# Expert gates scattered into a DRAM table by accumulating DMAs, and the up tiles' weights split on ScalarE and VectorE

## The reference, cut to what matters

```python
s1 = einsum('nhd,hkd->nhk', q[..., :half], k1)      # 128 row keys
s2 = einsum('nhd,hkd->nhk', q[..., half:], k2)      # 128 column keys
v1, i1 = top_k(s1, 16);  v2, i2 = top_k(s2, 16)
cand = v1[..., :, None] + v2[..., None, :]          # 256 candidates of a head
cidx = i1[..., :, None] * 128 + i2[..., None, :]
sv, pos = top_k(cand, 16)
idx = take_along_axis(cidx, pos)                    # 16 experts of a head
gate = softmax(sv)
act = gelu(einsum('nd,nhkd->nhk', h, u[idx]))
y = einsum('nhk,nhkd->nd', gate * act, v[idx])
```

## Time and profile before

| | |
|---|---|
| median of 3 runs | 2392.8 us (2392.65 to 2400.04) |
| profiled execution | 2399.22 us |
| its span, first to last instruction | 2397.4 us |
| mean granted clock of PE | 0.975 |
| busy: PE, PEld, DVE, ACT, POOL | 2316.3, 2238.5, 1566.4, 796.7, 1176.5 us |
| first up matmul, first down matmul, last down matmul | 860.6, 1764.3, 2380.2 us |

### The profile page before, as it was taken

How to read it: one execution, slowest core, us unless ns; L and a number is a source line. 1 busy time by engine, 2 the same in 40 slices (tenths; PEclk the granted TensorE clock), 3 DMA queues, 4 the chain that set the end, 5 groups by cost and what they waited for, 6 DMA issues and landing times.

```text
span 2397.4 us, 42364 instructions
## 1 busy us (share of the span) xinstructions
PE 2316.3 (97%) x15368; PEld 2238.5 (93%) x15368; DVE 1566.4 (65%) x2881; ACT 796.7 (33%) x1433; POOL 1176.5 (49%) x710
## 2 busy tenths in 40 slices
PE   7999999999999999999998999999999999999997
PEld 7899989898999999999998999999999999999996
DVE  6423723697765489999302777777657777787777
ACT  3212320564110011111112666666633332333332
POOL 4444341254554446666654444444454555565642
PEclk9999996899999999999998999999999999999998
DMA  6345345356554446663333444444489999999973
GB/s 199 117 143 156 117 134 184 109 162 216 181 187 145 140 148 206 210 193 127 129 128 135 151 178 179 179 179 179 179 301 308 312 331 306 339 309 332 316 253 129
DMA packets 318702, 475.27 MB, mean 198 GB/s; under 512 B 18448, under 2 KB 229008, under 8 KB 314784
## 3 DMA queue, kind: packets, MB, share of 16 engines
q1 hardware_dynamic: 185536, 256.47, 33.2%
q10 hardware_dynamic: 110560, 150.56, 18.6%
q0 software_dynamic: 22528, 67.19, 8.0%
HBM read 392.75 MB, written 148.52 MB: 226 GB/s over the span
## 4 chain that ended last, share of the span: by engine, by line
PE 83%; DVE 10%; issue 2%; ACT 2%; DMA 1%; ACTq 1%; POOL 0%; DVEq 0%; SPq 0%; POOLq 0%
PE ps L469 50%; PE ps L743 25%; PE ps L716 2%; PE ps L626 1%; PE ps L571 1%; PE ps L618 1%; DMA sr<-sig_scratch 1%; PE ps L675 1%; DVE xpad L1365 1%; ACT oh L1047 0%; DVE rstd L1449 0%; DVE rstd L1427 0%; PE ps L596 0%; DVE rr L1415 0%; PE ps L508 0%
## 5 line engine op out<-in xcount | busy, mean ns | idle before, releaser
L416 POOL TENSOR_SCALAR w_hi<-w_raw 128x1024 fp32r<-128x1024 f32 x225 | 261.9, 1164 | 901.3 <-issue 669.3
L419 POOL TENSOR_TENSOR w_lo<-w_raw,w_hi 128x1024 fp32r<-128x1024 f32 x225 | 579.6, 2576 | 18.8
L469 PE MATMUL ps<-n_hi,w_hi 128*128 128x288 f32 x2048 | 439.2, 296 | 7.7 <-DVE n_lo L1186 3.7
L469 PE MATMUL ps<-n_lo,w_hi 128*128 128x288 f32 x2048 | 439.4, 296 | 0.0
L469 PE MATMUL ps<-n_hi,w_lo 128*128 128x288 f32 x2048 | 439.0, 295 | 0.0
L743 PE MATMUL ps<-c_hi,w_lo 128*128 128x448 f32 x1024 | 371.7, 363 | 0.0
L743 PE MATMUL ps<-c_lo,w_hi 128*128 128x448 f32 x1024 | 371.1, 362 | 0.0
L743 PE MATMUL ps<-c_hi,w_hi 128*128 128x448 f32 x1024 | 368.9, 360 | 1.2 <-issue 0.8
L469 PEld LDWEIGHTS ps<-n_hi,w_hi 128*128 128x128 f32 x2048 | 327.0, 189 | 9.3 <-issue 4.8
L469 PEld LDWEIGHTS ps<-n_hi,w_lo 128*128 128x128 f32 x2048 | 330.7, 189 | 0.0
L469 PEld LDWEIGHTS ps<-n_lo,w_hi 128*128 128x128 f32 x2048 | 329.8, 189 | 0.0
(11 more groups left out here) (276 smaller groups left out, 3748.5 us busy)
## 6 DMA issues: line engine op xcount, KB each, us to landing
value_rows<-in_down SPq DMA_DIRECT2D x128, 512.0 KB, 5.3
w_raw<-in_up SPq DMA_DIRECT2D x128, 512.0 KB, 3.4
w_raw<-in_down SPq DMA_DIRECT2D x128, 512.0 KB, 6.6
w_raw<-in_trunk SPq DMA_DIRECT2D x96, 512.0 KB, 3.4
act_scratch<-ast ACTq DMA_DIRECT2D x128, 288.0 KB, 2.1
c_act<-act_scratch ACTq DMA_DIRECT2D x16, 1792.0 KB, 18.3
gate_scratch<-gst ACTq DMA_DIRECT2D x28, 1024.0 KB, 4.3
c_gate<-gate_scratch ACTq DMA_DIRECT2D x15, 1792.0 KB, 25.8
```

What stands on the lines that cost most here:

```text
L416: nc.gpsimd.tensor_scalar(w_hi[j % 2][:, :, :], w_raw[j][:, :, :], 1.0, 1.0, ALU.mult, ALU.mult).then_inc(w_hi_done, 1)
L419: nc.gpsimd.tensor_tensor(w_lo[j % 2][:, :, :], w_raw[j][:, :, :], f(w_hi[j % 2][:, :, :]), ALU.subtract).then_inc(w_split, 1)
L469: last = nc.tensor.matmul(ps[:, 2 * p + a, 0:w], wt[:, k, :], act[:, k, t0 + a * w:t0 + (a + 1) * w], start=k == 0 and part == 0, stop=k = ...
```

## The change

- **A cleared table.** POOL sets a tile of zeros once, and SP clears the table of gates (448 tokens x 16,384 experts, float32, 29.4 MB; now one row of 448 tokens for each expert) with 32 DMAs behind the loads and copies of trunk tiles 64 to 95.
- **Scatter.** The numbers of the cells are worked out by DVE (`cells`), and POOL adds each gate into the table by an indirect DMA with accumulation: one DMA for a chunk of tokens and one pick, 4 chunks x 128 picks = 512 DMAs (the fourth chunk has 64 tokens). Between the heads of a chunk POOL waits for the earlier head's DMAs to land; the chunks are staggered by three heads.
- **No expansion.** Transposes, one-hots, `gate_pair`, `gated`, `low_parts`, the 28 stores and the direct fill of `c_gate` go.
- **Splitting.** POOL splits tiles up to 105 (N_B = 106) alone. From tile 106 on ACT makes the high part and DVE the low part, as was done for the down tiles.
- **Top-k.** Chunk 0 runs as before; each of chunks 1 to 4 is interleaved with the low parts of 16 up tiles, and softmax and cells of the chunk before it are made inside. ACT makes the exponential chunk by chunk, behind the Gelu of up tiles 11, 27, 43, 59 and 75.
- **Loads.** ACT waits for all scatters behind up tile 119, and then loads the gates of the first two groups. A group's gates are now read as 8 rows of 448 numbers in one piece for each partition.

```diff
-            with pool.Fori(1, N_D // 4) as i:
+            with pool.Fori(1, N_CLEAR // 4 - 1) as i:
                 for j in range(4):
                     split(j, i * 4 + j)
+            pool.wait_ge(sig_stored, 16 * 3 * KT)
+            nc.gpsimd.memset(zeros[:, :], 0.0).then_inc(zeroed, 1)
...
+            def clear(k):
+                sp.dma_start(g_rows[:, ds(k * 4, 4), :], zeros[:, :].unsqueeze(1).to_broadcast([P, 4, TD])
+                             ).then_inc(cleared, 16)
+            def load_up(j, n):
+                sp.wait_ge(d_lo_done, n - (N_B + 3))
+                sp.dma_start(w_raw[j][:, :, :], up[ds(n - N_U, 1), :, :]...).then_inc(raw_in[j], 16)
...
+            def scatter_gates(c, h):
+                w = P if c < CD - 1 else DLAST
+                if h:
+                    pool.wait_ge(scattered[c], 16 * TOPK * h)
+                else:
+                    pool.wait_ge(cells_ready, c + 1)
+                for m in range(h * TOPK, (h + 1) * TOPK):
+                    nc.gpsimd.indirect_dma_start(
+                        g_cells, bass.IndirectOffsetOnAxis(ap=g_idx[0:w, c, m:m + 1], axis=0),
+                        chosen[0:w, c, 2, m:m + 1], None, compute_op=ALU.add).then_inc(scattered[c], 16)
...
+            pool.wait_ge(cleared, 16 * (NK // 4))
+            for step in range(PH + 3 * (CD - 1)):
+                for c in range(CD):
+                    if 0 <= step - 3 * c < PH:
+                        scatter_gates(c, step - 3 * c)
...
+            def split_high(j, n):
+                act.wait_ge(raw_in[j], (n - j) * 4 + 16)
+                act.wait_ge(tile_done, n - 1)
+                A(w_hi[j % 2][:, :, :], w_raw[j][:, :, :], ACT.Copy).then_inc(d_hi_done, 1)
...
+            begin = (N_B - 2 - N_U) // 4
+            up_tiles(0, begin, split=False)
+            for c in range(CT):
+                up_tiles(begin if c == 0 else 4 * c - 1, 4 * c + 3)
+                act.wait_ge(picked, c + 1)
+                A(chosen[:, c, 2, :], chosen[:, c, 2, :], ACT.Exp).then_inc(gate_exp, 1)
+            up_tiles(4 * CT - 1, NK // 4 - 2)
...
             act_load(0, 0)
+            for c in range(CD):
+                act.wait_ge(scattered[c], 16 * PICKS)
+            gate_load(0, 0)
+            gate_load(1, 1)
+            up_tiles(NK // 4 - 2, NK // 4 - 1)
...
+            def split_low(j, n):
+                dve.wait_ge(d_hi_done, n - (N_B - 1))
+                V.tensor_tensor(w_lo[j % 2][:, :, :], w_raw[j][:, :, :], f(w_hi[j % 2][:, :, :]), ALU.subtract
+                                ).then_inc(d_lo_done, 1)
+            def cells(i, then):
+                row = lambda side: chosen[:, ds(i, 1), side, :].rearrange("p o j -> p (o j)")
+                then(V.scalar_tensor_tensor(cell_f[:, :], row(1), float(NK), row(0), ALU.mult, ALU.add))
+                then(V.scalar_tensor_tensor(cell_f[:, :], cell_f[:, :], float(TD),
+                                            token[:, ds(i, 1)].to_broadcast([P, PICKS]), ALU.mult, ALU.add))
+                then(V.tensor_copy(g_idx[:, ds(i, 1), :].rearrange("p o j -> p (o j)"), cell_f[:, :]))
...
+            choose(0, 0, lambda: None)
+            with dve.Fori(1, CT) as i:
+                choose(i, i * STEPS + (FIRST_STEPS - STEPS), next_low, i - 1)
```

More of the change, by code:

```diff
@@ L55 @@
 NGB = TD // GB
[L56 to L59, removed]
 E1G = 8
@@ L386, in _ @@
                     copy_rows(i * 4 + (j - 4))
-            with sp.Fori(0, (NGRP * KT - N_U) // 4 + 1) as i:
+            sp.wait_ge(zeroed, 1)
+            with sp.Fori(N_CLEAR // 4, N_U // 4) as i:
+                for j in range(4):
+                    load(trunk, i, 0, j)
+                    copy_rows(i * 4 + (j - 4))
+                    clear(i * 4 + (j - N_CLEAR))
+            first_up = (N_B + 3 - N_U) // 4
+            with sp.Fori(0, first_up) as i:
                 for j in range(4):
@@ L698, in _ @@
             hn2 = lambda j: (n_hi, n_lo)
[L700 to L723, removed]
-                for j in range(4):
[L725 to L733, removed]
+            split_at = (N_B - N_U) // 4
+            stage(N_U, split_at * 4, hn2)
+            for j in range(4):
+                n = N_U + split_at * 4 + j
+                pe.wait_ge(pair_free[j % 2], n // 2 + 1)
+                product(j, n, n_hi, n_lo, j % 2, by_pool=n < N_B)
+            with pe.Fori(split_at + 1, NK // 4) as i:
+                for j in range(4):
+                    pe.wait_ge(pair_free[j % 2], i * 2 + (N_U // 2 + j // 2 + 1))
+                    product(j, i * 4 + (N_U + j), n_hi, n_lo, j % 2, by_pool=False)
             def down_tile(d, n, gg, ready=None, begin=False, end=False):
-                pe.wait_ge(d_lo_done, n - (N_D - 1))
+                pe.wait_ge(d_lo_done, n - (N_B - 1))
                 s = d % 2
@@ L1013, in _, with up_tile @@
             act.wait_ge(sc_copied, 3 * PH + 1)
-            def up_tiles(i0, i1, before=None, after=None):
+            def split_high(j, n):
+                act.wait_ge(raw_in[j], (n - j) * 4 + 16)
+                act.wait_ge(tile_done, n - 1)
+                A(w_hi[j % 2][:, :, :], w_raw[j][:, :, :], ACT.Copy).then_inc(d_hi_done, 1)
+            def up_tile(j, u):
+                act.wait_ge(tile_done, u + (N_U + 1))
+                act.wait_ge(a_stored[j], (u - j) * 4 + 16)
+                A(halves(ast[j][:, :]), opair(j % 2), ACT.Gelu).then_inc(pair_free[j % 2], 1)
@@ L1022, in up_tiles @@
[L1022 to L1056, removed]
-                        gated(q % RING, i * 2 * BQ + q)
@@ L1529, in _, with softmax, choose @@
             LOWEST = -3.4028235e38
-            STEPS = 21
-            with dve.Fori(0, CT) as i:
+            FIRST_STEPS, STEPS = 21, 27
+            def split_low(j, n):
+                dve.wait_ge(d_hi_done, n - (N_B - 1))
+                V.tensor_tensor(w_lo[j % 2][:, :, :], w_raw[j][:, :, :], f(w_hi[j % 2][:, :, :]), ALU.subtract
+                                ).then_inc(d_lo_done, 1)
+            V.tensor_tensor(cell_f[:, :], idt[:, :], iot[:, :], ALU.mult).then_inc(cell_step, 1)
+            dve.wait_ge(cell_step, 1)
+            V.tensor_reduce(token[:, 0:1], cell_f[:, :], AX, ALU.add).then_inc(cell_step, 1)
+            dve.wait_ge(cell_step, 2)
+            for c in range(1, CD):
+                V.tensor_scalar(token[:, c:c + 1], token[:, 0:1], float(c * P), None, ALU.add).then_inc(cell_step, 1)
+            dve.wait_ge(cell_step, CD + 1)
+            def softmax(i, then):
+                parts = chosen[:, ds(i, 1), 2, :].rearrange("p o (h k) -> p (o h) k", h=PH)
+                then(V.tensor_reduce(sm[:, 0, :], parts, AX, ALU.add))
+                then(V.reciprocal(sm[:, 0, :], sm[:, 0, :]))
+                then(V.tensor_tensor(parts, parts, sm[:, 0, :].unsqueeze(2).to_broadcast([P, PH, TOPK]), ALU.mult))
+            def cells(i, then):
[4 more added lines that the diff above has]
+                then(V.tensor_copy(g_idx[:, ds(i, 1), :].rearrange("p o j -> p (o j)"), cell_f[:, :]))
+            def choose(i, done, low, earlier=None):
                 n_top = [0]
@@ L1545, in best @@
                     then(last)
+                    low()
                     for q in range(n):
@@ L1557, in best @@
                     then(last)
+                    low()
                 then(V.tensor_copy(work[:, :, :], scores[:, ds(i, 1), :, :].rearrange("p o q k -> p (o q) k")))
                 best(2 * PH, lambda q: work[:, q, :], lambda q, s: tv[:, q, s:s + 8], lambda q, s: ti[:, q, s:s + 8])
+                if earlier is not None:
+                    dve.wait_ge(gate_exp, earlier + 1)
+                    softmax(earlier, then)
+                    cells(earlier, then)
+                    dve.sem_inc(cells_ready, 1)
+                    low()
                 V.tensor_copy(tif[:, :, :], ti[:, :, :])
```

241 lines of the change are left out of this document (105 added, 136 removed).

## The result

The changed kernel took 2650.97 us (median of 4 runs, 2648.28 to 2653.4) beside 2394.84 for the kernel before (4 runs, 2392.65 to 2400.04): ratio 1.107, 95% interval 1.104 to 1.109. It is slower by a tenth; the forecast was 2329 us, and its range ended at 2474.

The account below looks back on a forecast made before the run. PE, busy 97% of the span, was taken as the bound. From 2399.2 us profiled, 80 off PE and 16 added for standstill and lower clock gave 2335, or 2329 for the median; forecast 2313 to 2353, upward range to 2474.

Parts of the forecast that it names:

- the price of an accumulating DMA: POOL's scatter: each accumulating DMA costs a gather's 0.94 us undisturbed, 1.24 us rhythm, 1.37 us mean, ending at 1674 us.
- stretching: POOL's scatter: DMAs starting inside DVE operations with two SBUF inputs wait for them, 1.47 us a DMA during the top-k.
- The rival that came true: POOL's scatter: accumulating DMAs cost more than gathers, so it ends late and eats the gain; up to 2474 us, chance 0.25.
- Its bound: Upper price for POOL's scatter DMAs: the down stage's mean, 1.61 us each, PE standing 153 us, 2474 us total.
- Landings in series: POOL's scatter: each DMA waits for the one before to land, 3.9 us each; above 3600 us, chance 0.03.
- The 64-row DMAs: Fourth chunk's 128 scatter DMAs: save 60 us if the price goes by rows, nothing if it is fixed.
- What leaves PE: Up stage on PE: gate matmuls and the pause go, 80.0 us less, with up tiles at 6.41 us.
- The split: Up tiles' split on ACT and DVE: 85 us of DVE work a chunk fits 102.6 us, costed at nothing.
- the third rival: Up stage: DVE becomes the pace of the up tiles; at 110 us a chunk, 30 us more, 2343 us, chance 0.08.
- Clearing: 32 table-clearing DMAs on SP's queue between weight loads: 3.9 us each at most, taken as nothing, bounds 0 and 8 us.
- the fourth: Clearing (8 us) or first gates (some 15 us at the first down tile) exposed; 2328 us, chance 0.07.
- The first gates and the down stage: First gate loads fit in the 38 us of tiles 122 to 127; the down stage stays 616 us.

Follow-up runs that it names:

- experiment seven: As experiment six, with the 64-token last chunk scattered two picks of a head per DMA over 128 partitions, 448 DMAs; 2326.07 us, ratio 0.971.
- experiment six: Changed kernel with plain scatters, VectorE adding earlier gates of the same token and cell, 20 low parts a chunk, head order written out; 2376.2 us, ratio 0.992.
- experiment five: Changed kernel, still accumulating, with VectorE's up-tile low parts taking their second operand from PSUM instead of SBUF; 2600.41 us, ratio 1.086.
- experiment one: Changed kernel with its 512 scatters writing plainly instead of accumulating, so earlier gates in a shared cell are lost; 2333.98 us, ratio 0.975.
- two: Changed kernel with 512 plain gathers from the cleared table into the tile of gates in place of the scatters; 2331.28 us in one run.
- eight: Changed kernel with its scatters turned into 512 accumulating gathers from the cleared table into SBUF; 2649.58 us in one run.

## Why the prediction was wrong

**The step that failed** is the price of an accumulating DMA. The forecast took a gather's 0.94 us for it, because gathers of 4 and of 4096 bytes cost the same. Its sum had 549 us of DMAs: 512 x 1.373 us, less 512 x 0.30 us of idle time. Plain scatters measured 530.5, so for them the term was right within 4%; of it the forecast had 68 us as stretching (549 - 512 x 0.94), and 47 were found. Accumulating ones measured 854.2. Of the 323.7 us between those, 384 x 0.58 + 128 x 0.52 = 289 are the undisturbed price, 1.54 against 0.96 us for 128 rows and 1.42 against 0.90 for 64; the other 34 are what is left, put down to more stretching: the 102 DMAs that start in a split lose 0.7 us each, the 106 plain ones that do so 0.24. With the start 7 us early and the waits 3 us shorter, the end moves from 1674 by 305 - 10 = 295 us, to 1968.4.

**The rival that came true** is the first, an accumulating DMA that costs POOL more, given 0.25. Its rule of 51 us for each 0.1 us fits: the mean interval was (1968.4 - 944.75 - 13.9) / 512 = 1.97 us, 0.60 above the forecast's 1.37, so 307 us. Its bound did not fit. It took 1.61 us from the median of L438 in the down stage, but that median is the same 0.94 us stretched by splits. It bounded the disturbance once more and not the new operation. The rival's own argument, that an accumulation reads and writes, would have given twice 0.94 plus 0.30, or 2.18 us, and a range that held the result.

**Landings in series** are excluded: DMAs start 1.85 us apart and land after 2.9 in the median. They do not take twice as long either; the waits between heads were 13.9 us where the forecast had 19 and feared 20 more. (The Trainium skill, "DMA: Bandwidth & Descriptors", section "Anatomy of one DMA — SWDGE (gpsimd) path", puts most of its fixed 2.0 us into completion and calls descriptor generation small; here completions overlap and POOL's own 0.96 or 1.54 us for each DMA set the pace.)

**The 64-row DMAs** save 0.12 us each, 15 us in all and not the 60 of a price by rows: the price is nearly fixed. One of the last chunk's, when it is scattered alone:

```profile
1854.22 1.42 POOL L453 DMA_INDIRECT gate_scratch<-chosen,g_idx  x1 [0.30 <-issue]
```

**What leaves PE** came as worked out, and some more: splits start 6.35 us apart, so a tile is 0.06 us shorter than 6.41, 7.6 us over the stage. The first up tile also ended 8.8 us earlier in this execution, by Gelu's first table load at 860.58 instead of 869.4 us. That may be chance: the first up matmul starts at 860.0 us in the kernel before (not at the table's 860.6), at 852.6 here, and between 850.9 and 858.1 us over all nine profiles of changed forms. Both bring forward the moment at which PE runs out of work, 1630.5 instead of 1645 us. From the forecast's span of 2397.4 - 80 + 16 = 2333.4 us: + 330.8 for a standstill of 342.8 instead of 12, - 7.6 - 8.8 = 2647.8 of the 2648.0 measured. The six tiles behind the pause took 41.4 us instead of 38.1; some 2.3 of that are the lower clock, at which 20 matmuls started 0.24 us apart instead of 0.13. The forecast allowed 4.

**The split cost nothing**, as forecast, and DVE did not become the pace (the third rival): of PE's 343.3 us of waiting for low parts 0.5 are not the one standstill, and the top-k ended at 1316 us, not 1329. **Clearing cost nothing** either (the fourth). All engines of the changed kernel from 627 to 860 us, columns as in the earlier trace rows:

```profile
627.00:860.00 233.00, 226.97 (x1699) 223.39 (x1698) 135.04 (x154) 22.56 (x33) 116.82 (x64) 0.99 0.80 264
```

The DMA share went from 0.50 to 0.80 and PE's busy time stayed. The working beneath was off, though: a clear lands after 8.1 us in the median, not 3.9.

```profile
gate_scratch<-zeros SPq DMA_DIRECT2D x32, 896.0 KB, 8.1
```

**The first gates and the down stage** were right:

```profile
L756 PE MATMUL ps<-c_hi,w_hi x1024: 359/360/472, 2014.7 to 2629.9; 128*128 128x448 f32 x171
```

It is 615.2 us from first to last start, 615.5 in the earlier trace rows. Of the gates, asked for at 1970 us, DVE multiplied the first at 1997.3 us, before PE began at 2014.7.

## What to carry to other kernels

A DMA form that the trace does not hold has no price from its nearest relative: bound it from above by what it does more (here it reads as well as writes, so twice; it measured 1.54 against 0.94 us, and no run tests the bound on another form), or leave the accumulation out, as experiment seven does by adding collisions up on an engine with room. When many small DMAs stand between two stages, multiply first: 512 of them turn 0.6 us into 300, and packing two half-filled ones into one (50 us from experiment six to seven) was worth as much as taking away what stretches them (51 us in experiment five). Where a wait names an engine that was long done, or "issue", look for the queue's own wait in front of it.

## What was not expected of the hardware

An accumulating indirect DMA keeps POOL busy for 1.54 us against 0.94 to 0.96 without, in either direction (experiments one, two and eight). A VectorE operation of the same shape, 1.22 us, holds up none of POOL's DMAs once one of its inputs is in PSUM (experiment five). And POOL falls into step with the splits: with 1.84 us from start to start, three DMAs and one stretch of some 0.8 us fill exactly one tile of 6.35 us, so that one in three was stretched and not the share that evenly spread starts would give.

One difference that the trace shows goes unexplained. The pages count the packets of POOL's DMA queue (packets, MB, share of 16 engines), here the changed kernel and experiment one:

```profile
q0 software_dynamic: 88064, 67.45, 14.3%
...
q0 software_dynamic: 38912, 67.45, 8.6%
```

The kernel before has 22528, so for the same bytes 512 accumulating DMAs made 65536 packets and 512 plain ones 16384. In the trace an accumulating DMA moves each row in a packet of its own, of 4 bytes, where a plain one of 128 rows moves eight rows in one of 32 bytes. That this is what POOL spends the 0.58 us on is not shown, and the number of packets alone does not do it: the gathers of 4096-byte rows also make a packet for each row, and POOL spends 0.94 us on one.
